# Loading x as columns, and its rows later, at the start of a two-layer decoder trunk

## The chip, the cores and the metric

One NeuronCore of a Trainium2 chip runs the whole program, one launch. The metric is the device time of that launch in microseconds, the median of several runs. A profiled execution is a run of its own, with its own time.

## The reference

Two layers over 256 tokens of width 1024, float32. Each layer is a half-step SwiGLU sub-layer, a token-mixing sub-layer (windowed attention and latent attention, gated), and a second half-step SwiGLU. The change touches the first SwiGLU of the first layer alone:

```
def rms_norm(x, g):
    y = x * rsqrt(mean(x * x, axis=-1) + 1e-6)
    return y * g
for l in range(2):
    x = x + 0.5 * (silu(h @ w_gate) * (h @ w_up)) @ w_down      # h = rms_norm(x, ffn1_norm[l])
    ...
```

w_gate and w_up are 1024 x 2816, w_down is 2816 x 1024.

## The kernel before

Every float32 operand of a matmul is split in two float32r parts, high (a rounded copy, made by ScalarE) and low (the rest, a subtraction on VectorE). A product is then three matmul passes: high by high, high by low, low by high. A SwiGLU runs over 22 blocks of 128 hidden columns. For a block the gate's and the up part's weights (a `gu` block, 1 MB) stand still in TensorE and the normalised x streams through. TensorE contracts over its partitions, so x has to lie with its 1024 channels on partitions: 8 "columns" of 128 channels by 256 tokens, in `hT` (high and low beside each other, so that one 512-wide matmul, `high`, does high weight by both parts of x; `low`, 256 wide, does low weight by high x). Only the gain goes into `hT`. The factor 1/rms of a token, `rs`, is left out there and comes in afterwards: `spread_rs` on TensorE (two transposes, L1410 to L1415) spreads it over the partitions, ScalarE copies it to `rsB` (L627 to L630), and VectorE multiplies the gate's sum by it (`gate_scaled`, L953). From there silu, the product with the up part, its split into `aTh` and `aTl`, and the twelve matmuls of the down block (`down`, L1576) follow.

At the program's start nothing is on the chip. SyncE issues all loads from one queue in the order of the code (L316 to L323, L360 to L362): x in two halves, with the gains (`cols`) in front of the first; block 0's weights in four pieces of 256 KB (`start_cols(i)`: gate or up by i % 2, channels 0 to 511 or 512 to 1023 by i // 2); block 1's in two pieces of 512 KB; block 0's down weights `d0`; block 2's weights into `SG` (`third_raw`); and `d1`. Later loads wait until VectorE has read the buffer that they fill.

x comes with tokens on partitions. TensorE therefore transposes it (`column_start`, L1396, 16 matmuls with the identity into PSUM), ScalarE makes the high part (`columns_high`, L610) and VectorE the low part (`columns_low`, L1006), both reading the transposed x from PSUM. Until x is there TensorE multiplies a constant (`keep_warm`, L1380). Each engine runs its instructions in the order in which the code issues them, and semaphores (`start_hi`, `ht_lo`, ...) tie the engines together. ScalarE's order is L705 to L719, VectorE's L1076 to L1083 and then `ffn`, TensorE's `gate_up_start` (L1523), `gate_up_second`, `gate_up_third`, `down`. In `gate_up_start` a group of four `high` matmuls (`start_high_four(s, half)`; s is 0 for gate, 1 for up) is followed by its four `low`.

The sum of squares of x is made from x by rows, on ScalarE (L718) and VectorE (L897). VectorE finishes the mean (L932, L934), GpSimd the power -1/2 (L465). `spread_rs` stands after the fifth `high` matmul of block 1's up part (L1553).

Of the kernel before, what the change touches and what calls it, by code (L numbers as in the profile page):

```python
# [14 lines left out]
P = 128  # L15
# [46 lines left out]
X_AT_FIRST = ((2, 0), (3, 0), (4, 0), (6, 0), (5, 0), (7, 0), (2, 1), (3, 1))  # L62
X_AT = ((2, 0), (3, 0), (4, 0), (6, 0), (2, 1), (3, 1), (5, 0), (7, 0))
RS_BANK = 5
COLS_PAD = 32
# [32 lines left out]
def build(nc, x_first_in, x_second_in, pos_in, cols_in, rows_in, w_ffn, w_proj, w_gate, w_uq, w_ukv, w_branch, w_out,  # L98
          masks_in, freq_in, out):
    with ExitStack() as ctx:  # L100
# [31 lines left out]
        qkB_PT = sb("qkB_PT", [P, 2 * TT * HB * QKB])  # L132
        qB = qkB_PT[:, 0:TT * HB * QKB].rearrange("p (t n) -> p t n", t=TT)
        kB_rows = qkB_PT[:, TT * HB * QKB:]
        kB = qkB_PT[:, TT * HB * QKB:].rearrange("p (t n) -> p t n", t=TT)
        PT = qkB_PT[:, :].rearrange("p (h n) -> p h n", h=HB)
# [18 lines left out]
        x_cols = sb("x_cols", [P, COLS_PAD + TT * D_MODEL])  # L155
        x = x_cols[:, COLS_PAD:].rearrange("p (h t n) -> p h t n", h=2, t=TT)
        cols = x_cols[:, 0:7 + 3 * KC]
# [51 lines left out]
        ht_ps = signal("ht_ps", 3 * KC)  # L209
# [14 lines left out]
        x_in_done = [signal(f"x_in_done{h}", 0) for h in range(2)]  # L224
# [81 lines left out]
        def x_place(layer, n, c):  # L306

            bank, half = (X_AT_FIRST if layer + n == 0 else X_AT)[c]
            return ps[:, bank, half * SEQ:(half + 1) * SEQ]
# [5 lines left out]
        def _(sp):  # L315
            part = slice(0, COLS_PAD + TT * HALF)  # L316
            sp.dma_start(x_cols[:, part], x_first_in).then_inc(x_in_done[0].sem, 16)  # L317
            sp.dma_start(x_cols[:, COLS_PAD + TT * HALF:], x_second_in).then_inc(x_in_done[1].sem, 16)  # L318
            for i in range(4):
                sp.dma_start(raw_gu[0][:, start_cols(i)], w_ffn[0, :, start_cols(i)]).then_inc(start_in[i].sem, 16)  # L320
            for s, sem in enumerate((start_in[4].sem, raw_gu_in[1].sem)):
                part = slice(s * KC * P, (s + 1) * KC * P)
                sp.dma_start(raw_gu[1][:, part], w_ffn[1, :, part]).then_inc(sem, 16)  # L323

# [24 lines left out]
            def load_ffn_first(l, w):  # L349
                for b in range(2):  # L350
                    if w == 1:
                        sp.wait_ge(lo_gu.sem, lo_gu.at(l, MIX0 + OUT + 1 + b))
                    elif l > 0:
                        sp.wait_ge(lo_gu.sem, lo_gu.at(l - 1, FFN2_0 + FB - 2 + b))
                    if l + w > 0:
                        load_gu((2 * l + w) * FB + b, b)
                    if l > 0 and w == 0 and b == 0:
                        load_last_d(l - 1, 1)
                if l == 0 and w == 0:
                    load_d(0, 0)  # L360
                    sp.dma_start(third_raw, w_ffn[2, :, 0:GU_COLS]).then_inc(third_in.sem, 16)
                    load_d(1, 1)  # L362
                    return
                for b in range(2):
                    if w == 1:
                        sp.wait_ge(lo_gu.sem, lo_gu.at(l, MIX0 + OUT + 3))
                    else:
                        sp.wait_ge(lo_d.sem, lo_d.at(l - 1, 2 * FB - 2 + b))
                    load_d((2 * l + w) * FB + b, b)
# [58 lines left out]
        def _(pool):  # L428
# [11 lines left out]
            pool.wait_ge(x_in_done[0].sem, 16)  # L440
            pool.sem_inc(small_in.sem, 16)
            pool.wait_ge(x_in_done[1].sem, 16)
# [77 lines left out]
        def _(act):  # L520
# [4 lines left out]
            for l in range(DEPTH):  # L525
# [80 lines left out]
                def columns_high(n, part=range(KC)):  # L606
                    act.wait_ge(small_in.sem, small_in.per_layer * (l + 1))
                    for c in part:
                        act.wait_ge(ht_ps.sem, ht_ps.at(l, KC * n + c))
                        act.activation(hTh[:, c, :], x_place(l, n, c), ACT.Copy,  # L610
                                       scale=cols[:, 7 + n * KC + c:8 + n * KC + c]).then_inc(ht_hi.sem, 1)
# [93 lines left out]
                if l == 0:  # L705
                    columns_high(0, range(0, 4))
                    start_high(0)
                    columns_high(0, range(4, 6))
                    start_high(1)
                    columns_high(0, range(6, 8))  # L710
                    start_high(2)
                    start_high(3)
                    for s, (landed, sig) in enumerate(((start_in[4], start_hi), (raw_gu_in[1], hi_gu))):
                        part = slice(s * KC * P, (s + 1) * KC * P)
                        act.wait_ge(landed.sem, 16)
                        act.activation(wh_gu[1][:, part], raw_gu[1][:, part], ACT.Copy).then_inc(sig.sem, 1)
# [152 lines left out]
        def _(dve):  # L869
# [3 lines left out]
            for l in range(DEPTH):  # L873
# [12 lines left out]
                def split_second(n):  # L886

                    for half, sig in enumerate((lo_first, lo_gu)):
# [7 lines left out]
                        if n + half == 0:  # L896
# [105 lines left out]
                def columns_low(n, part=range(KC), layer=l):  # L1002
                    dve.wait_ge(small_in.sem, small_in.per_layer * (layer + 1))
                    for c in part:
                        dve.wait_ge(ht_hi.sem, ht_hi.at(layer, KC * n + c))
# [361 lines left out]
        def _(pe):  # L1367
# [15 lines left out]
            keep_warm(7)  # L1383
            pe.wait_ge(ident_set.sem, 2)
            for l in range(DEPTH):
# [9 lines left out]

                def column_start(c):  # L1396

                    if c >= 6:
                        pe.wait_ge(ht_lo.sem, ht_lo.at(0, c - 6))
                    dst = x_place(0, 0, c)  # L1400
                    for t in range(TT):
                        ins = pe.transpose(dst[:, t * P:(t + 1) * P], x[:, c // 4, t, c % 4 * P:(c % 4 + 1) * P], ident[:, :])
                    ins.then_inc(ht_ps.sem, 1)
# [119 lines left out]
                def gate_up_start():  # L1523

                    pe.wait_ge(x_in_done[0].sem, 16)
                    for c in range(4):
                        column_start(c)
                    keep_warm(1)
                    pe.wait_ge(x_in_done[1].sem, 16)
                    for c in range(4, KC):  # L1530
                        column_start(c)
                    start_high_four(0, 0)
                    start_low_four(0, 0)
                    start_high_four(1, 0)
                    start_low_four(1, 0)
                    start_high_four(0, 1)
                    start_low_four(0, 1)
                    start_high_four(1, 1)
                    start_low_four(1, 1)

                def gate_up_second(w):

                    for s, sig in enumerate((gate_ps, gu_used)):
# [16 lines left out]
                        ins.then_inc(sig.sem, 1)  # L1560
                def gate_up_third():
# [423 lines left out]
```

## Time and profile before

| what | us |
|---|---|
| runs of the kernel before | 1039.35, 1039.02, 1038.98; median 1039.02 |
| the profiled execution's own time | 1039.14 |
| its span, first to last instruction | 1037.3 |
| TensorE (PE) busy with matmuls | 1032.0, 99% of the span |
| VectorE (DVE) busy | 717.8, 69% |
| ScalarE (ACT) busy | 586.5, 57% |
| GpSimd (POOL) busy | 65.5, 6% |
| loads: mean rate over the span | 181 GB/s, 187.53 MB |
| the first fortieth of the span, 25.9 us | 264 GB/s, engines of the DMA busy 7 tenths |

A busy time says how long an engine had something under way. A timeline row gives start, length, engine, line, operation and tiles (out<-in), how often, and in brackets how long the engine had been idle before and what ended that. The chain of waits follows the end of the program back to its start. A DMA row gives the time from issue to landing. The granted clock is TensorE's; it has two levels here, 1.00 (2.4 GHz) and 0.50 (1.2 GHz).

### The profile page before, as it was taken

The numbers are of one execution on the slowest core, as the hardware profiler recorded it, in microseconds if no ns is written. First come the engines' busy times: TensorE is split into PE (matmuls) and PEld (weight loads), VectorE is DVE, ScalarE is ACT, GpSimd is POOL, SyncE is SP. The second block draws the span as 40 slices with busy tenths as digits, with TensorE's granted clock in tenths as the row PEclk, the third lists the DMA queues.
The fourth block names the chain that finished last, engine by engine and source line by source line (L and its number), as shares of the span: only waits on it lengthen the run. The fifth ranks groups of instructions, "written<-read, shape, count | busy, mean of one in ns | idle before, by whom it ended". The sixth has DMA issues, their size and how long they took to land.

```text
span 1037.3 us, 15559 instructions
## 1 busy us (share of the span) xinstructions
PE 1032.0 (99%) x5648; PEld 892.2 (86%) x5648; DVE 717.8 (69%) x1132; ACT 586.5 (57%) x935; POOL 65.5 (6%) x71
## 2 busy tenths in 40 slices
PE   9999999999999999999999999999999999999998
PEld 7888888998888888888888888889988888888887
DVE  6766676668786876666687666666697868676665
ACT  7545454457864755454565455455688646454552
POOL 0052000122100000000000000001211000000000
PEclk9999999999999999999999999999999999999999
DMA  7665544455335555655545555634454346546551
GB/s 264 249 227 192 203 163 166 141 184 207 131 123 203 177 190 185 207 191 204 181 146 204 200 194 180 214 132 155 153 204 162 122 162 222 203 162 202 190 174 61
DMA packets 35269, 187.53 MB, mean 181 GB/s; under 512 B 4368, under 2 KB 4384, under 8 KB 20128
## 3 DMA queue, kind: packets, MB, share of 16 engines
q1 hardware_dynamic: 34992, 186.51, 51.6%
q0 software_dynamic: 240, 0.53, 0.2%
q8 instruction: 23, 0.38, 0.1%
q14 instruction: 14, 0.11, 0.0%
HBM read 185.98 MB, written 1.05 MB: 180 GB/s over the span
## 4 chain that ended last, share of the span: by engine, by line
PE 99%; DMA 1%; SPq 0%; DVE 0%; ACT 0%; issue 0%
PE ps L1369 96%; PE ps L1803 1%; PE ps L1393 1%; DMA w_raw<-in_w_ffn 1%; PE ps L1832 1%; PE ps L1868 0%; PE ps L1712 0%; PE ps L1704 0%; PE ps L1414 0%; DVE x_cols L999 0%; ACT w_hi L554 0%; SPq L318 0%; SPq L317 0%
## 5 line engine op out<-in xcount | busy, mean ns | idle before, releaser
L1369 PE MATMUL ps<-hT,w_hi 128*128 128x512 f32 x1408 | 341.2, 391 | 0.9 <-ACT w_hi L554 0.9
L1369 PEld LDWEIGHTS ps<-hT,w_hi 128*128 128x128 f32 x1408 | 258.9, 188 | 51.4 <-ACT w_hi L554 1.1
L884 DVE TENSOR_TENSOR w_lo<-w_raw,w_hi 128x2048 fp32r<-128x2048 f32 x82 | 188.0, 2292 | 87.4 <-ACT w_hi L549 87.4
L1369 PEld LDWEIGHTS ps<-hT,w_lo 128*128 128x128 f32 x1408 | 176.7, 188 | 7.5
L1369 PE MATMUL ps<-hT,w_lo 128*128 128x256 f32 x1408 | 178.3, 279 | 0.0
L1369 PE MATMUL ps<-w_hi,hT 128*128 128x512 f32 (+2 forms) x576 | 173.5, 376 | 0.0
L549 ACT ACTIVATE w_hi<-w_raw 128x2048 fp32r<-128x2048 f32 x85 | 161.9, 1905 | 13.6 <-PE ps L1369 13.2
L1369 PE MATMUL ps<-w_lo,aTh 128*128 128x512 f32 x352 | 137.1, 390 | 0.0
L1369 PE MATMUL ps<-w_hi,aTl 128*128 128x512 f32 x352 | 137.0, 389 | 0.0
L1369 PE MATMUL ps<-w_hi,aTh 128*128 128x512 f32 x352 | 136.8, 390 | 0.0
L578 ACT ACTIVATE S<-ps 128x256 f32<-128x256 f32 x88 | 33.7, 383 | 155.4 <-PE ps L1369 155.4
L1369 PEld LDWEIGHTS ps<-w_hi,hT 128*128 128x128 f32 x576 | 107.2, 188 | 14.8
L878 DVE TENSOR_TENSOR w_lo<-w_raw,w_hi 128x2048 fp32r<-128x2048 f32 (+3 forms) x50 | 94.8, 1903 | 29.8 <-ACT w_hi L537 29.6
L572 ACT ACTIVATE w_hi<-w_raw 128x1024 fp32r<-128x1024 f32 x88 | 92.8, 1055 | 38.5 <-PE ps L1369 38.5
L537 ACT ACTIVATE w_hi<-w_raw 128x2048 fp32r<-128x2048 f32 (+3 forms) x54 | 86.0, 1593 | 49.0 <-PE ps L1369 47.0
L1369 PE MATMUL ps<-w_lo,hT 128*128 128x512 f32 (+2 forms) x288 | 107.5, 373 | 0.0
L940 DVE TENSOR_TENSOR w_lo<-w_raw,w_hi 128x1024 fp32r<-128x1024 f32 x88 | 104.3, 1218 | 1.4 <-ACT w_hi L572 1.4
L946 DVE TENSOR_TENSOR S<-ps,S 128x256 f32<-128x256 f32 x88 | 37.0, 420 | 85.4 <-ACT S L578 85.4
L1369 PEld LDWEIGHTS ps<-w_hi,aTl 128*128 128x128 f32 x352 | 66.1, 188 | 13.9
L1369 PEld LDWEIGHTS ps<-w_hi,aTh 128*128 128x128 f32 x352 | 66.1, 188 | 13.6
L1369 PEld LDWEIGHTS ps<-w_lo,aTh 128*128 128x128 f32 x352 | 66.1, 188 | 13.0
L584 ACT ACTIVATE work<-work 128x256 f32<-128x256 f32 x88 | 36.7, 418 | 68.1 <-DVE work L953 68.1
(168 smaller groups left out, 956.9 us busy)
## 6 DMA issues: line engine op xcount, KB each, us to landing
w_raw<-in_w_ffn SPq DMA_DIRECT2D x85, 1024.0 KB, 5.0
w_raw<-in_w_ffn SPq DMA_DIRECT2D x90, 512.0 KB, 5.8
w_raw<-in_w_gate SPq DMA_DIRECT2D x16, 1024.0 KB, 4.9
w_raw<-in_w_proj SPq DMA_DIRECT2D x16, 592.0 KB, 4.3
w_raw<-in_w_branch SPq DMA_DIRECT2D x8, 1024.0 KB, 4.9
w_raw<-in_w_out SPq DMA_DIRECT2D x8, 1024.0 KB, 4.9
w_raw<-in_w_uq SPq DMA_DIRECT2D x4, 384.0 KB, 3.1
w_raw<-in_w_ffn SPq DMA_DIRECT2D x4, 256.0 KB, 6.2
```

The source lines that it names most:

```text
L537: act.activation(mix_hi[m][:, 0:ncols], mix_raw[m][:, 0:ncols], ACT.Copy).then_inc(hi_gu.sem, 1)
L549: act.activation(wh_gu[b], raw_gu[b], ACT.Copy).then_inc(hi_gu.sem, 1)
L572: act.activation(wh_d[b], raw_d[b], ACT.Copy).then_inc(hi_d.sem, 1)
L578: act.activation(folded[:, b, 0, :], ps[:, 2 * b, SEQ:2 * SEQ], ACT.Copy).then_inc(g_low.sem, 1)
L584: act.activation(silu[:, b, :], silu[:, b, :], ACT.Silu).then_inc(silu_done.sem, 1)
L878: dve.tensor_tensor(mix_lo[m][:, 0:ncols], mix_raw[m][:, 0:ncols], mix_hi[m][:, 0:ncols].bitcast(F32), ALU.subtract).then_inc(lo_gu.sem, 1)
L884: dve.tensor_tensor(wl_gu[b], raw_gu[b], wh_gu[b].bitcast(F32), ALU.subtract).then_inc(lo_gu.sem, 1)
L940: dve.tensor_tensor(wl_d[b], raw_d[b], wh_d[b].bitcast(F32), ALU.subtract).then_inc(lo_d.sem, 1)
L946: dve.tensor_tensor(folded[:, b, 0, :], ps[:, 2 * b, 0:SEQ], folded[:, b, 0, :], ALU.add)\
L1369: return pe.matmul(dst, w, m, start=start, stop=stop, skip_group_check=True)
L1393: ins = pe.transpose(dst[:, t * P:(t + 1) * P], x[:, c // 4, t, c % 4 * P:(c % 4 + 1) * P], ident[:, :])
L1803: ins = pe.transpose(ps[:, 4 + h % 4, s * P:(s + 1) * P], S[:, h, s * P:(s + 1) * P], ident[:, :])
```

## The change

The host lays x out a second time, as columns (`xt_first`, channels 0 to 511, with the gains behind it; `xt_second`, channels 512 to 1023). In the first sub-layer of the first layer, ScalarE and VectorE split these columns straight from SBUF; the 16 transposes, the PSUM places for them and their waits are gone there. `xt_first` goes out first, `xt_second` behind the first of block 0's four pieces. x by rows, 1024 KB in one load, goes out behind block 1's weights; both sums of squares wait for it, on VectorE now behind both halves of block 1's low part. Block 2's weights go out ahead of `d0`. ScalarE's order of columns and pieces changes, and VectorE's. TensorE runs two groups of `high` (gate, up) and then two of `low`, for each half of the channels, `spread_rs` stands behind the whole of block 1, and the constant is multiplied 10 times, not 7 and 1. The columns lie where `qB`, `kB` and `PT` are put later, and a pad moves those.

```diff
-        ht_ps = signal("ht_ps", 3 * KC)
+        ht_ps = signal("ht_ps", 3 * KC, -KC)
...
         def x_place(layer, n, c):
-            bank, half = (X_AT_FIRST if layer + n == 0 else X_AT)[c]
+            if layer + n == 0:
+                return xt(c)
+            bank, half = X_AT[c]
...
-            part = slice(0, COLS_PAD + TT * HALF)
-            sp.dma_start(x_cols[:, part], x_first_in).then_inc(x_in_done[0].sem, 16)
-            sp.dma_start(x_cols[:, COLS_PAD + TT * HALF:], x_second_in).then_inc(x_in_done[1].sem, 16)
+            sp.dma_start(xt_first, xt_first_in).then_inc(xt_in[0].sem, 16)
             for i in range(4):
+                if i == 1:
+                    sp.dma_start(xt_second, xt_second_in).then_inc(xt_in[1].sem, 16)
                 sp.dma_start(raw_gu[0][:, start_cols(i)], w_ffn[0, :, start_cols(i)]).then_inc(start_in[i].sem, 16)
...
+            sp.dma_start(x_cols[:, cols_at + COLS_PAD:], x_in).then_inc(x_in_done.sem, 16)
...
                 if l == 0 and w == 0:
+                    sp.dma_start(third_raw, w_ffn[2, :, 0:GU_COLS]).then_inc(third_in.sem, 16)
                     load_d(0, 0)
-                    sp.dma_start(third_raw, w_ffn[2, :, 0:GU_COLS]).then_inc(third_in.sem, 16)
                     load_d(1, 1)
...
-            pool.wait_ge(x_in_done[0].sem, 16)
+            pool.wait_ge(xt_in[0].sem, 16)
             pool.sem_inc(small_in.sem, 16)
-            pool.wait_ge(x_in_done[1].sem, 16)
+            pool.wait_ge(x_in_done.sem, 16)
             pool.sem_inc(x_done.sem, 2 * TT)
...
                 if l == 0:
-                    columns_high(0, range(0, 4))
+                    columns_high(0, range(0, 2))
                     start_high(0)
-                    columns_high(0, range(4, 6))
+                    columns_high(0, range(2, 4))
                     start_high(1)
-                    columns_high(0, range(6, 8))
+                    columns_high(0, range(4, 8))
                     start_high(2)
                     start_high(3)
...
                     act.wait_ge(ss_clear.sem, 1)
+                    act.wait_ge(x_in_done.sem, 16)
...
-                        if n + half == 0:
+                        if n == 0 and half == 1:
+                            dve.wait_ge(x_in_done.sem, 16)
...
                 if l == 0:
                     columns_low(0, range(0, 4))
                     start_low(0)
-                    columns_low(0, range(4, 6))
                     start_low(1)
-                    columns_low(0, range(6, 8))
+                    columns_low(0, range(4, 8))
                     start_low(2)
                     start_low(3)
...
-            keep_warm(7)
+            keep_warm(10)
...
                 def gate_up_start():
-                    pe.wait_ge(x_in_done[0].sem, 16)
-                    for c in range(4):
-                        column_start(c)
-                    keep_warm(1)
-                    pe.wait_ge(x_in_done[1].sem, 16)
-                    for c in range(4, KC):
-                        column_start(c)
-                    start_high_four(0, 0)
-                    start_low_four(0, 0)
-                    start_high_four(1, 0)
-                    start_low_four(1, 0)
-                    start_high_four(0, 1)
-                    start_low_four(0, 1)
-                    start_high_four(1, 1)
-                    start_low_four(1, 1)
+                    for half in range(2):
+                        for s in range(2):
+                            start_high_four(s, half)
+                        for s in range(2):
+                            start_low_four(s, half)
...
                             high(2 + s, wh_gu[1][:, c:c + P], k, k == 0)
-                            if l + w == 0 and s == 1 and k == 4:
-                                spread_rs(0)
...
+                    if l + w == 0:
+                        spread_rs(0)
```

`columns_high` and `columns_low` wait for the landing of the half that column c lies in (`xt_in[c // 4]`) where they waited for the transposes.

SyncE's queue from the program's start, before: x's two halves are ahead of all weights, and `SG` is block 2.

```order
L317 DMA x_cols<-in_x_first 128x1056
L318 DMA x_cols<-in_x_second 128x1024
L320 DMA w_raw<-in_w_ffn 128x512 x4
L323 DMA w_raw<-in_w_ffn 128x1024 x2
L347 DMA w_raw<-in_w_ffn 128x1024
L361 DMA SG<-in_w_ffn 128x2048
L347 DMA w_raw<-in_w_ffn 128x1024
```

The same queue now:

```order
L328 DMA x_cols<-in_xt_first 128x1056
L332 DMA w_raw<-in_w_ffn 128x512
L331 DMA x_cols<-in_xt_second 128x1024
L332 DMA w_raw<-in_w_ffn 128x512 x3
L335 DMA w_raw<-in_w_ffn 128x1024 x2
L336 DMA x_cols<-in_x 128x2048
L373 DMA SG<-in_w_ffn 128x2048
L360 DMA w_raw<-in_w_ffn 128x1024 x2
```

One weight piece has moved ahead of the second half of x, and 1024 KB have come in ahead of block 2 and both down blocks.

TensorE from its first matmul to the second group of `low`, before (`hT`,`w_hi` 512 wide is a `high`, `hT`,`w_lo` 256 wide a `low`):

```order
L1380 MATMUL ps<-kTA 128x128 [waits warm_set]
L1380 MATMUL ps<-kTA 128x128 x6
L1402 MATMUL ps<-ident,x_cols 128x128 [waits x_in_done0,ident_set]
L1402 MATMUL ps<-ident,x_cols 128x128 x7
L1380 MATMUL ps<-kTA 128x128
L1402 MATMUL ps<-ident,x_cols 128x128 [waits x_in_done1]
...
L1369 MATMUL ps<-hT,w_hi 128x512 [waits ht_lo,start_hi]
L1369 MATMUL ps<-hT,w_hi 128x512 [waits ht_lo] x3
L1369 MATMUL ps<-hT,w_lo 128x256 [waits start_lo]
L1369 MATMUL ps<-hT,w_lo 128x256 x3
L1369 MATMUL ps<-hT,w_hi 128x512 [waits start_hi]
```

The same place now:

```order
L1399 MATMUL ps<-kTA 128x128 [waits warm_set]
L1399 MATMUL ps<-kTA 128x128 x9
L1388 MATMUL ps<-hT,w_hi 128x512 [waits ht_lo,start_hi,ident_set]
L1388 MATMUL ps<-hT,w_hi 128x512 [waits ht_lo] x3
L1388 MATMUL ps<-hT,w_hi 128x512 [waits start_hi]
L1388 MATMUL ps<-hT,w_hi 128x512 x3
L1388 MATMUL ps<-hT,w_lo 128x256 [waits start_lo]
L1388 MATMUL ps<-hT,w_lo 128x256 x3
```

The transposes are gone, and the second group of `high`, with its wait for the second weight piece, stands ahead of the first `low`.

VectorE from block 0's last low piece to the first use of `rsB` (`S`,`rsB`), before:

```order
L894 TENSOR_TENSOR w_lo<-w_raw,w_hi 128x1024 [waits start_hi]
L897 SCALAR_TENSOR_TENSOR sq,ss<-x_cols 128x1024
L932 TENSOR_TENSOR rs_step<-ss 128x2 [waits ss_done]
L934 TENSOR_SCALAR rs_step<-rs_step 128x2 [waits ms_sum]
L894 TENSOR_TENSOR w_lo<-w_raw,w_hi 128x1024 [waits hi_gu]
L946 TENSOR_TENSOR S<-ps,S 128x256 [waits g_low]
L964 TENSOR_TENSOR S<-ps,S 128x256 [waits u_low]
L908 TENSOR_TENSOR w_lo<-SG,w_hi 128x1024 [waits third_hi]
L953 TENSOR_TENSOR work<-S,rsB 128x256 [waits gate_sum,rsb_done]
```

The same place now:

```order
L911 TENSOR_TENSOR w_lo<-w_raw,w_hi 128x1024 [waits start_hi]
L911 TENSOR_TENSOR w_lo<-w_raw,w_hi 128x1024 [waits hi_gu]
L915 SCALAR_TENSOR_TENSOR sq,ss<-x_cols 128x1024 [waits x_in_done]
L950 TENSOR_TENSOR rs_step<-ss 128x2 [waits ss_done]
L952 TENSOR_SCALAR rs_step<-rs_step 128x2 [waits ms_sum]
L964 TENSOR_TENSOR S<-ps,S 128x256 [waits g_low]
L982 TENSOR_TENSOR S<-ps,S 128x256 [waits u_low]
L926 TENSOR_TENSOR w_lo<-SG,w_hi 128x1024 [waits third_hi]
L971 TENSOR_TENSOR work<-S,rsB 128x256 [waits gate_sum,rsb_done]
```

The sum of squares has moved behind the second low half, and it waits for a load.

## Rows read from the trace of the kernel before

**Rows 1.** The page: busy time of each engine.

```profile
PE 1032.0 (99%) x5648; PEld 892.2 (86%) x5648; DVE 717.8 (69%) x1132; ACT 586.5 (57%) x935; POOL 65.5 (6%) x71
```

**Rows 2.** The chain of waits in order of time: start us, us, what.

```profile
1.65 5.90 DMA w_raw<-in_w_ffn
...
7.57 0.64 ACT w_hi L554
...
8.26 9.82 PE ps L1369 x53
```

**Rows 3.** Timeline, TensorE in the first block, the second, and a later one.

```profile
8.26 1.20 PE L1369 MATMUL ps<-hT,w_hi 128*128 128x512 f32 x4 [0.86 <-ACT w_hi L554]
...
13.96 2.03 PE L1369 MATMUL ps<-hT,w_hi 128*128 128x512 f32 x8
...
30.78 3.80 PE L1369 MATMUL ps<-hT,w_hi 128*128 128x512 f32 x16
...
34.42 2.03 PE L1369 MATMUL ps<-hT,w_lo 128*128 128x256 f32 x16
...
36.28 0.40 PE L1369 MATMUL ps<-w_hi,aTh 128*128 128x512 f32 x1
```

**Rows 4.** Timeline: when three of the first loads were issued.

```profile
1.18 0.43 SPq L318 DMA_DIRECT2D x_cols<-in_x_second  x1
...
2.12 0.43 SPq L320 DMA_DIRECT2D w_raw<-in_w_ffn  x1
...
5.54 0.65 SPq L361 DMA_DIRECT2D SG<-in_w_ffn  x1
```

**Rows 5.** DMA issues, these three: size, median us from issue to landing.

```profile
x_cols<-in_x_second SPq DMA_DIRECT2D x1, 512.0 KB, 4.5
...
w_raw<-in_w_ffn SPq DMA_DIRECT2D x1, 256.0 KB, 6.1
...
SG<-in_w_ffn SPq DMA_DIRECT2D x1, 1024.0 KB, 10.3
```

**Rows 6.** Timeline: TensorE's first transpose, at the landing of x's first half.

```profile
4.62 1.36 PE L1402 MATMUL ps<-ident,x_cols 128*128 128x128 f32 x8 [0.21 <-DMA x_cols<-in_x_first]
```

**Rows 7.** Groups by line, ACT and DVE, 0 to 17 us: busy us, mean ns.

```profile
L610 ACT ACTIVATE hT<-ps,x_cols 128x256 fp32r<-128x256 f32 x8 | 3.2, 472 | 3.2 <-PE ps L1402 3.2
L554 ACT ACTIVATE w_hi<-w_raw 128x512 fp32r<-128x512 f32 x4 | 2.4, 636 | 0.6 <-DMA w_raw<-in_w_ffn 0.6
...
L917 DVE TENSOR_TENSOR w_lo<-w_raw,w_hi 128x512 fp32r<-128x512 f32 x4 | 2.7, 685 | 0.6 <-ACT w_hi L554 0.6
```

**Rows 8.** The same work from SBUF: one line each, duration ns min/median/max.

```profile
L597 ACT ACTIVATE aTh<-work x88: 396/398/419, 20.7 to 1030.1; 128x256 fp32r<-128x256 f32 x88
...
L984 DVE TENSOR_TENSOR aTl<-work,aTh x88: 412/418/619, 21.8 to 1030.5; 128x256 fp32r<-128x256 f32 x88
```

**Rows 9.** Timeline: the chain of `rs`, and block 1's last split ahead of its `down`.

```profile
13.35 1.22 DVE L897 SCALAR_TENSOR_TENSOR sq<-x_cols 128x1024 f32<-128x1024 f32 x1
...
15.06 1.62 POOL L465 TENSOR_TENSOR rs<-rs_step,minus_half 128x2 f32<-128x2 f32 x1 [13.14 <-DVE rs_step L934]
...
17.91 0.38 PE L1414 MATMUL ps<-ident,rs 128*128 128x128 f32 x2
...
24.93 0.42 DVE L984 TENSOR_TENSOR aTl<-work,aTh 128x256 fp32r<-128x256 f32 x1
...
28.06 0.39 PE L1369 MATMUL ps<-w_hi,aTh 128*128 128x512 f32 x1
```

**Rows 10.** Timeline: TensorE's constants at the start, and its last matmul.

```profile
1.05 3.35 PE L1380 MATMUL ps<-kTA 128*128 128x128 f32 x14 [1.05 <-DVE kTA L870]
...
5.82 0.39 PE L1380 MATMUL ps<-kTA 128*128 128x128 f32 x2
...
1033.74 0.39 PE L1369 MATMUL ps<-w_hi,aTl 128*128 128x512 f32 x1
```

**Rows 11.** Windows at the end: engines' busy us, granted clock, DMA share, GB/s.

```profile
1036.10:1037.30 1.20, 0.00 (x0) 0.00 (x0) 0.00 (x0) 0.00 (x0) 0.00 (x0) 0.50 0.31 119
```

More of the change, by code:

```diff
@@ L61 @@
 Q_BANK, K_BANK = (4, 5, 6), (7, 0, 1)
-X_AT_FIRST = ((2, 0), (3, 0), (4, 0), (6, 0), (5, 0), (7, 0), (2, 1), (3, 1))
 X_AT = ((2, 0), (3, 0), (4, 0), (6, 0), (2, 1), (3, 1), (5, 0), (7, 0))
 RS_BANK = 5
-COLS_PAD = 32
+COLS_PAD, PT_FRONT, PT_BACK = 32, 48, 16
+PT_COLS = 2 * TT * HB * QKB
 PROJ_GROUPS = ((0, 384), (384, 768), (768, PROJ_COLS))
@@ L95, in at, with build @@
         return layer * self.per_layer + (k + 1 + self.first)
-def build(nc, x_first_in, x_second_in, pos_in, cols_in, rows_in, w_ffn, w_proj, w_gate, w_uq, w_ukv, w_branch, w_out,
+def build(nc, xt_first_in, xt_second_in, x_in, pos_in, cols_in, rows_in, w_ffn, w_proj, w_gate, w_uq, w_ukv, w_branch, w_out,
           masks_in, freq_in, out):
@@ L131, in build @@
         kTA = sb("kTA", [P, SEQ])
[L132 to L136, printed above, removed]
         qTB = sb("qTB", [P, 6, SEQ])
@@ L154, in build, with xt @@
         trig = sb("trig", [P, 2, TT, 16])
-        x_cols = sb("x_cols", [P, COLS_PAD + TT * D_MODEL])
-        x = x_cols[:, COLS_PAD:].rearrange("p (h t n) -> p h t n", h=2, t=TT)
-        cols = x_cols[:, 0:7 + 3 * KC]
+        x_cols = sb("x_cols", [P, PT_FRONT + PT_COLS + PT_BACK + COLS_PAD + TT * D_MODEL])
+        qkB_PT = x_cols[:, PT_FRONT:PT_FRONT + PT_COLS]
+        qB = qkB_PT[:, 0:TT * HB * QKB].rearrange("p (t n) -> p t n", t=TT)
+        kB_rows = qkB_PT[:, TT * HB * QKB:]
+        kB = qkB_PT[:, TT * HB * QKB:].rearrange("p (t n) -> p t n", t=TT)
+        PT = qkB_PT.rearrange("p (h n) -> p h n", h=HB)
+        cols_at = PT_FRONT + PT_COLS + PT_BACK
+        x = x_cols[:, cols_at + COLS_PAD:].rearrange("p (h t n) -> p h t n", h=2, t=TT)
+        cols = x_cols[:, cols_at:cols_at + 7 + 3 * KC]
+        xt_first = x_cols[:, cols_at - KC // 2 * SEQ:cols_at + COLS_PAD]
+        xt_second = x_cols[:, PT_FRONT:PT_FRONT + KC // 2 * SEQ]
+        def xt(c):
+            half, i = divmod(c, KC // 2)
+            return (xt_first, xt_second)[half][:, i * SEQ:(i + 1) * SEQ]
         rows = sb("rows", [P, 2 * ROPE + HA])
@@ L223, in build @@
         rows_in_done = signal("rows_in_done", 16)
-        x_in_done = [signal(f"x_in_done{h}", 0) for h in range(2)]
+        xt_in = [signal(f"xt_in{h}", 0) for h in range(2)]
+        x_in_done = signal("x_in_done", 0)
         start_in = [signal(f"start_in{i}", 0) for i in range(5)]
@@ L608, in columns_high @@
                     for c in part:
-                        act.wait_ge(ht_ps.sem, ht_ps.at(l, KC * n + c))
+                        if l + n == 0:
+                            act.wait_ge(xt_in[c // (KC // 2)].sem, 16)
+                        else:
+                            act.wait_ge(ht_ps.sem, ht_ps.at(l, KC * n + c))
                         act.activation(hTh[:, c, :], x_place(l, n, c), ACT.Copy,
@@ L1004, in columns_low @@
                     for c in part:
+                        if layer + n == 0:
+                            dve.wait_ge(xt_in[c // (KC // 2)].sem, 16)
                         dve.wait_ge(ht_hi.sem, ht_hi.at(layer, KC * n + c))
@@ L1394, in transposed @@
                         ins.then_inc(ht_ps.sem, 1)
[L1396 to L1403, printed above, removed]
                 def columns(layer, n, h):
@@ L1959 @@
     cols = gain_cols[0]
-    x_halves = a["x"].reshape(TT, P, 2, HALF).transpose(2, 1, 0, 3).reshape(2, P, TT * HALF)
+    x_rows = a["x"].reshape(TT, P, 2, HALF).transpose(1, 2, 0, 3).reshape(P, TT * D_MODEL)
+    xt_halves = a["x"].reshape(SEQ, 2, KC // 2, P).transpose(1, 3, 2, 0).reshape(2, P, KC // 2 * SEQ)
     arrays = {
-        "x_first": np.concatenate([cols, np.zeros((P, COLS_PAD - cols.shape[1]), f32), x_halves[0]], axis=1),
-        "x_second": x_halves[1],
+        "xt_first": np.concatenate([xt_halves[0], cols, np.zeros((P, COLS_PAD - cols.shape[1]), f32)], axis=1),
+        "xt_second": xt_halves[1],
+        "x": x_rows,
         "positions": a["positions"],
```

## The prediction

> **What bounds the kernel now.** I read the page's engine shares first: TensorE has a matmul under way in 99% of the span, every other engine has room [rows 1]. The chain of waits, from its start, says where TensorE is not yet the bound: a weight load until 7.55 us, ScalarE's high part of that piece until 8.21, and from 8.26 on TensorE alone [rows 2]. So only what comes before 8.26 us, and a new wait behind it, can change the time. The timeline then tells how full TensorE is in block 0: 16 `high` and 16 `low` run from 8.26 to 13.96, 5.70 us; with nothing to wait for, in a later block, 16 `high` take 34.42 - 30.78 = 3.64 and 16 `low` 36.28 - 34.42 = 1.86, together 5.50 [rows 3]. Block 0 thus stalls 0.20 us in all, and the whole head that can be won is the 8.26 us ahead of it.
>
> **The loads.** The sum of bytes in front of a load sets when it lands. Block 0's second piece (gate and up alternate, so it is the first up piece) has 528 + 512 + 256 + 256 = 1552 KB up to its end and lands at 2.12 + 6.1 = 8.2 us; block 2's weights end at 4624 KB and land at 5.54 + 10.3 = 15.8 [rows 4, 5]. That is 3072 KB in 7.6 us, 0.64 us for 256 KB, 2.55 for 1024. x's first half was there just ahead of 4.62 [rows 6], its second at 1.18 + 4.5 = 5.7 [rows 4, 5]. The first piece, 256 KB behind that, landed only at 7.55 [rows 2]: 1.9 us where the rate makes it 0.64, so some 1.2 us were lost there once.
>
> In the new order the first piece ends at 784 KB. At the rate alone it lands 0.64 us behind 4.5, at 5.1; with the same loss, at 6.3. The second half of the columns ends at 1296 KB, and the second piece again at 1552 KB: the same sum as before, and I take the same landing, **8.2 us**. (If the loss is gone, 7.0. I take the row of the same sum, since the piece that lost the time still comes first among the weights.) Everything up to block 1's weights keeps its sum. x by rows ends at 4112 KB: 15.8 - 512 KB (1.27) = 14.6 us. Block 2 ends at 5136 KB instead of 4624, +1.3, 17.1 us; `d0` about 18.4, `d1` 19.7.
>
> The Trainium skill, "DMA: Bandwidth & Descriptors", section "Latency and other measured facts", puts the access latency of HBM at 0.2 us on average and up to 2 us at high load. By that the 1.2 us are of a size that the load on the memory alone could make, at any place of the queue; no row here says which it was.
>
> **TensorE's block 0.** The 16 transposes and their PSUM reads go, but they ended ahead of 8.26 beside the load, so on the path they cost nothing by themselves. ScalarE's columns now come from SBUF: a 128x256 copy there takes 398 ns against 472 from PSUM, VectorE's 128x256 two-input operation 418 [rows 7, 8]. One after the other they start some 0.3 to 0.35 us apart (estimate: the duration less the 0.1 that neighbours overlap). Step by step: the columns are there at 4.5; GpSimd passes the gains' signal on, which I put at 0.2 us (no row shows it exposed; it only has to be ready by 5.4). ScalarE makes columns 0 and 1 until 5.5, waits for the first piece (5.1 to 6.3), needs 0.64 for it [rows 7]: TensorE's first real matmul starts at 5.9 to **7.0**, against 8.26. Columns 2 and 3 follow on ScalarE and VectorE until 8.2. Then comes the second piece: landing 8.2, high part 8.2 to 8.9. TensorE's second group waits for that, and since the new order puts it ahead of the first `low`, they wait behind it too. From 8.9 there is left: 12 `high` at 3.64/16 and 16 `low` at 1.86/16 [rows 3], 2.73 + 1.86 = 4.6, end at **13.5**, if ScalarE and VectorE keep ahead. ScalarE: columns 4 to 7 until 10.2, third piece until 10.8, fourth until 11.3; TensorE wants them at 10.7 and 11.6. VectorE: 0.685 for a piece [rows 7], low second piece until 9.6, columns until 11.0, last low piece until 12.2, wanted at 13.0. Both fit within 0.2 us. Gain: 13.96 - 13.5 = **0.4 to 0.5 us**. So what is won at the front is mostly taken back by the second piece, whose landing the change does not move.
>
> **The sum of squares and `rs`.** VectorE now waits for x until 14.6, and its low part of block 1 stands ahead of that wait, so nobody on TensorE waits for it. Queued behind are the folds of block 0's sums, first wanted by block 2's matmuls at 19. Squares 14.6 to 15.8 (1.22); from their end to GpSimd 15.06 - 14.57 = 0.5; the power 1.62 [rows 9]: `rs` at 17.9. TensorE comes to `spread_rs` behind block 1, 13.5 + 5.5 = 19.0. It has 1.1 us to spare: cost nothing; if x lands over 1.1 us later than 14.6, that is late next. The two transposes themselves (0.38) [rows 9] are moved, not removed. Block 2's weights, 17.1, are split by 18.2 for its first `high` at 19.2: cost nothing, 1 us to spare.
>
> Moved behind block 1, `rsB` comes 19.0 - 17.91 = 1.1 us later [rows 9], while TensorE is 0.45 earlier. The chain that hangs on it ends in `aTl` of block 1, done at 25.35, wanted by its `down` at 28.06 [rows 9]: 2.7 us to spare become 1.15. Cost nothing. The 1024 KB more delay `d0` by 5 us and `d1` by 2.6, which were 6 and 4 us early at ScalarE; the loads behind them are released by VectorE's reads and come about 1 us later, with several us to spare at TensorE.
>
> **The sum.** -0.45 us, nothing added. The profiled execution took 1039.14 us, 1.8 more than its span and 0.12 more than the median of 1039.02; against the median the forecast is **1038.6 us**. Less than 0.2% (2.08 us, about what a measurement of this kernel can tell from no change) either way.
>
> **The rivals.**
> *The second piece lands early.* If the 1.2 us were the place's and not the piece's, it lands at 7.0, TensorE is full from 7.7 and ends block 0 at 12.3: -1.6, **1037.4**. x then lands at 13.4, `rs` at 16.7, `spread_rs` is wanted at 17.8. Block 2, 15.9, just fits. For it: the rate before and behind is even. Against it: the slow place lies where the weights begin. With a part of the loss, times between 1037.4 and 1038.6. Chance 0.20.
>
> *TensorE's clock falls at the start.* Place: between the constants and block 0. Now the constants (14 rows in 3.35 us, 0.24 each, while two of the same at 5.82 take 0.39 together) and the transposes keep TensorE busy until 0.86 us ahead of 8.26 [rows 3, 10]. With the change 20 rows of constants end at about 5.7, and from there to 8.9 TensorE does four `high`, under 1 us of work. The trace's end shows a fall: the last matmul ends at 1033.74 + 0.39 = 1034.1, and in the window from 1036.1 the granted clock is 0.50, 1.2 GHz [rows 10, 11]. So some 2 us without a matmul were enough there. It decides if the first piece lands at 6.3, not at 5.1. Price: at the start TensorE worked some 4 us at the slow pitch before it went up [rows 10]; as long again from 8.9 does 2 us less work, block 0 ends at 15.5, +1.55, **1040.5**; a shorter fall gives 1039.5, and all of block 0 at the slow clock (+4.6 - 0.45) 1043.2. Against it: those were idle us, here some work lies in between. Chance 0.30.
> The Trainium skill, "TensorE: Matmul & The Clock Gate", section "HAM oscillation — how this bites in real kernels", has this case: a TensorE that waits for loads between short bursts of matmuls falls back to the half clock and pays at each burst. The trace's end agrees that it falls, 1036.1; whether bursts prevent it no row shows.
>
> *`rsB` comes too late.* The 1.15 us at block 1's `down` and the 1.1 at `spread_rs` are both worked out from loads that have not run in this order. If x lands 2 us late, TensorE stalls 0.9 at `spread_rs` and 0.5 to 1 at that `down`: +1.1, **1040.1**. Against it: the loads' rate is even. Chance 0.08.
>
> **How the numbers follow.** Forecast 0.40 (own range 1038.1 to 1039.0), early second piece 0.20, clock 0.30, late `rsB` 0.08, none of these 0.02. From 1037.3 to 1040.7 the range leaves out the worse half of the clock's case and little at the lower end. Faster by over 0.2% (under 1036.9) needs more than the largest gain that I can work out, 1.6: 0.03. Slower by over 0.2% (over 1041.1) needs the clock's worst end or two late chains: 0.06. Within: 0.91.
>
> **What would show it.** Right: the second piece's high part starts at about 8.2 and TensorE's second group at 8.9, block 1 begins at 13.5, x lands near 14.6, GpSimd's power starts at 16.3, `spread_rs` waits for nothing, `down` of block 1 neither, and the granted clock stays 1.00. `high` matmuls some 0.43 apart behind 8.9 would show the clock's case; the second piece at 7.0 the early one; idle time of TensorE ahead of `spread_rs` or that `down` the late one. Wrong altogether: a gain or a loss that arises behind 30 us, where I see the same work with time to spare.

## The result, and the profile after

| | before | changed |
|---|---|---|
| median of 22 runs each, us | 1038.99 | 1040.61 |
| lowest and highest | 1038.09, 1040.09 | 1038.67, 1042.39 |
| profiled execution, span, us | 1037.3 | 1039.4 |

The changed kernel is slower: ratio 1.0015, 95% interval 1.0009 to 1.0022. That is within the 0.2% called "no change", and within the range, but on the other side of the forecast of 1038.6.

The runs of the changed kernel lie 3.7 us apart, those of the kernel before 2.0, and the mean granted clock of a run sorts them: 5 runs at 1.000 have a median of 1039.42, 14 at 0.998 one of 1040.68, 3 at 0.996 one of 1042.10. Of the 55 runs of the kernel before beside the experiments, two took 1415 and 2106 us and are left out of every comparison; the others list a clock of 1.000, one of them 0.999.

The page, engines' shares: TensorE is as busy as before [rows 1], over a longer span.

```profile
PE 1031.9 (99%) x5636; PEld 892.0 (86%) x5636; DVE 718.5 (69%) x1132; ACT 587.4 (57%) x935; POOL 64.6 (6%) x71
```

The chain of waits from the start (start us, us, what) still begins with a weight load and goes on with TensorE [rows 2], but the load is now the second piece, and it lands at 9.05.

```profile
2.12 6.93 DMA w_raw<-in_w_ffn
...
9.07 0.64 ACT w_hi L567
...
9.76 12.02 PE ps L1388 x60
```

The timeline of TensorE in block 0 and at block 1's first matmul answers to [rows 3]:

```profile
1.05 3.91 PE L1399 MATMUL ps<-kTA 128*128 128x128 f32 x20 [1.05 <-DVE kTA L887]
...
5.93 0.70 PE L1388 MATMUL ps<-hT,w_hi 128*128 128x512 f32 x2 [0.97 <-DVE hT L1026]
...
6.87 0.90 PE L1388 MATMUL ps<-hT,w_hi 128*128 128x512 f32 x2 [0.24 <-DVE hT L1026]
...
9.76 1.19 PE L1388 MATMUL ps<-hT,w_hi 128*128 128x512 f32 x4 [1.99 <-ACT w_hi L567]
...
12.43 2.87 PE L1388 MATMUL ps<-hT,w_hi 128*128 128x512 f32 x8
...
15.13 1.10 PE L1388 MATMUL ps<-hT,w_lo 128*128 128x256 f32 x8
...
16.08 1.99 PE L1388 MATMUL ps<-hT,w_hi 128*128 128x512 f32 x8
```

The first real matmul starts 2.3 us earlier than before, and block 1 begins 2.1 us later, at 16.08 against 13.96. The eight `high` from 12.43 take 2.7 us until the next group; at the pace of [rows 3] they take 1.8. The windows say why (busy us of PE, PEld, DVE, ACT, POOL, then the granted clock, DMA share, GB/s):

```profile
8.00:9.00 1.00, 0.00 (x0) 0.00 (x0) 0.00 (x0) 0.00 (x0) 0.00 (x0) 1.00 1.06 418
9.00:10.00 1.00, 0.24 (x1) 0.24 (x2) 0.26 (x1) 0.93 (x2) 0.00 (x0) 1.00 1.03 418
10.00:10.80 0.80, 0.80 (x5) 0.63 (x5) 0.80 (x3) 0.80 (x3) 0.00 (x0) 1.00 1.06 435
10.90:14.20 3.30, 3.30 (x14) 2.91 (x13) 3.18 (x6) 3.30 (x6) 0.00 (x0) 0.50 1.03 436
14.30:15.00 0.70, 0.70 (x5) 0.56 (x4) 0.70 (x2) 0.00 (x0) 0.00 (x0) 1.00 1.00 421
```

From 10.9 to 14.2 us the granted clock is 0.50, 1.2 GHz. Ahead of that TensorE had ended its constants at 4.96 and had then done four `high`, with waits of 0.97 and 0.24 us, until it stood still for 2 us (to 9.76).

Behind block 0 nothing changed. From block 1's first `high` to the end of the span it is 1037.3 - 13.96 = 1023.3 us before and 1039.4 - 16.08 = 1023.3 now. So the whole question is when block 0 ends.

The loads, issue to landing, answer to [rows 5]; they were issued at 1.65, 2.12 and 4.98 us:

```profile
x_cols<-in_xt_second SPq DMA_DIRECT2D x1, 512.0 KB, 6.7
...
w_raw<-in_w_ffn SPq DMA_DIRECT2D x1, 256.0 KB, 6.9
...
x_cols<-in_x SPq DMA_DIRECT2D x1, 1024.0 KB, 10.4
```

The first weight piece, issued at 1.18, took 3.7 us and landed at 4.9, so nothing was lost on it. The columns' second half lands at 8.4, 3.5 us behind it, where the rate gives 1.3. The slow stretch has moved to that load and grown, and everything behind is 0.8 us late: second piece 9.05 (forecast 8.2), x 15.4 (14.6).

### The profile page after: what moved, and what is told of

Read it like the earlier page. It is cut to its first block, busy times and chain, and to the rows that moved or that the text cites. A ratio compares the mean times of both kernels' runs of the same rounds, so it can differ in the third digit from the quotient of the medians.

```text
span 1039.4 us, 15542 instructions
## 1 busy us (share of the span) xinstructions
PE 1031.9 (99%) x5636; PEld 892.0 (86%) x5636; DVE 718.5 (69%) x1132; ACT 587.4 (57%) x935; POOL 64.6 (6%) x71
## 4 chain that ended last, share of the span: by engine, by line
PE 99%; DMA 1%; SPq 0%; DVE 0%; ACT 0%; issue 0%
PE ps L1388 96%; PE ps L1804 1%; PE ps L1412 1%; DMA w_raw<-in_w_ffn 1%; PE ps L1833 1%; PE ps L1869 0%; PE ps L1713 0%; PE ps L1705 0%; PE ps L1424 0%; DVE x_cols L1017 0%; ACT w_hi L567 0%; SPq L332 0%; SPq L331 0%; SPq L328 0%
```

## The experiments

Two theories stood against each other. **Theory 1**: the clock falls, since TensorE has too little to do while it waits for the second piece, and the late landing costs 0.4 us besides. **Theory 2**: the new order of the groups, waiting for the late piece, is the whole loss. A separate pair, A and B, is about the slow stretch in the loads. All kernels below are the changed one with the edit shown; each was compared with the kernel before in the same session.

### e1_fill: keep TensorE at work while it waits

```diff
-            keep_warm(10)
+            keep_warm(12)
...
                             start_high_four(s, half)
+                            if half + s == 0:
+                                keep_warm(8)
```

> The changed kernel with constants multiplied 12 times at the start and 8 times more between TensorE's first and second group of block 0, where it waits 2 us for the second weight piece. Theory 1 (the clock falls because TensorE does too little between 5 and 9.8 us, worth 3.41 us at half speed = 1.7 us): granted clock 1.00 up to the last matmul in every run, block 0 ends at 14.4 instead of 16.1, median 1039.2 to 1039.5. Theory 2 (the order of the groups and the late second piece alone cost the time): nothing gained, 1040.6.

Measured: 1039.54 (11 runs, 1039.10 to 1039.85), ratio 1.0007, interval 0.9998 to 1.0016. Ten runs have a mean clock of 1.000, one 0.999. The same windows as above:

```profile
10.00:10.80 0.80, 0.80 (x7) 0.75 (x6) 0.80 (x3) 0.80 (x3) 0.00 (x0) 1.00 1.08 446
10.90:14.20 3.30, 3.30 (x21) 2.80 (x20) 3.19 (x6) 2.74 (x4) 0.00 (x0) 1.00 1.02 428
```

TensorE's second group, and block 1's first:

```profile
9.22 1.17 PE L1388 MATMUL ps<-hT,w_hi 128*128 128x512 f32 x4
...
14.16 2.01 PE L1388 MATMUL ps<-hT,w_hi 128*128 128x512 f32 x8
```

21 matmuls run in the stretch where the changed kernel has 14. Theory 1 holds and Theory 2 falls: the queue and the order of the groups are those of the changed kernel, the only edit is work that nobody uses, and 1.07 us are back. (In this profile the second piece landed at 8.45, not 9.05, so that 14.16 is no test of the 14.4 expected; the five runs of the changed kernel whose clock stayed up, 1039.42, are as fast as these.) The constants fill two waits, the one ahead of TensorE's first real matmul and the one for the second piece; which of the two the clock needed, this run does not tell. The 0.6 us left over the kernel before lie within this run's interval.

### e2_alternate: high and low alternating again

```diff
                             start_high_four(s, half)
-                        for s in range(2):
                             start_low_four(s, half)
```

> The changed kernel with high and low groups alternating again, as in the kernel before. Theory 1: the first low group (0.47 us, its operand is ready at 7.83) moves into the 2 us wait for the second piece, so 0.5 us less from that; whether the clock then still falls is open, since only 0.5 us more work lies ahead of 9.8: 1040.1 if it falls, 1039.0 if not. Theory 2 (the order of the groups is the whole loss): back to the kernel before, 1039.0 with the clock as it was in the changed kernel.

Measured: 1039.48 (1038.35 to 1040.84), ratio 1.0008, 0.9999 to 1.0017. Ten of 11 runs have a clock of 1.000 (median 1039.40), one 0.998 (1040.84). So the one `low` group in the wait is mostly enough to keep the clock, and the median lies between the two values given for Theory 1. By itself this run does not tell the theories apart, and one run at 0.998, 1.4 us above that median, is too little to do so. Its profile had the second piece early, at 7.5, and block 0 ended at 13.21:

```profile
5.87 1.84 PE L1388 MATMUL ps<-hT,w_hi 128*128 128x512 f32 x4 [0.18 <-DVE hT L1026]
7.81 0.74 PE L1388 MATMUL ps<-hT,w_lo 128*128 128x256 f32 x4
8.39 1.09 PE L1388 MATMUL ps<-hT,w_hi 128*128 128x512 f32 x4
...
13.21 2.03 PE L1388 MATMUL ps<-hT,w_hi 128*128 128x512 f32 x8
```

The `low` at 7.81 runs where the changed kernel waits. The span was 1036.5, 1023.3 behind block 0's end again, the shortest of all profiles. That is no gain over the kernel before: the profiled run took 1038.35, and 6 of the 31 runs of the kernel before made beside it were as short (1038.02 to 1038.35).

### e3_issue_late: issue fewer loads at once

```diff
+            sp.wait_ge(start_in[1].sem, 16)
             for s, sem in enumerate((start_in[4].sem, raw_gu_in[1].sem)):
```

> The changed kernel, SyncE waits for the landing of the second weight piece before it issues block 1's weights and all behind. Theory A (loads that are still being issued slow the ones under way: the slow packets end when SyncE has issued its last load, 6.7 us before and 7.5 us with the change): the columns' second half lands at 6.2, the second piece at 6.9, block 0 ends near 12.5, 1037.5 to 1038. Theory B (the slow stretch belongs to the time since the start, or to the third load of the queue): they land at 8.4 and 9.05 as before, block 1 a little later, 1040.6 or more.

Measured: 1040.53 (1039.19 to 1041.73), ratio 1.0017, 1.0008 to 1.0026; 3 of 11 runs at a clock of 1.000 (median 1039.31), 7 at 0.998 (1040.80), one at 0.996 (1041.73). The third and fourth load (issued at 1.65 and 2.12) took as long as ever:

```profile
x_cols<-in_xt_second SPq DMA_DIRECT2D x1, 512.0 KB, 6.4
...
w_raw<-in_w_ffn SPq DMA_DIRECT2D x1, 256.0 KB, 6.6
```

They landed at 8.0 and 8.7, not at 6.2 and 6.9. Theory A falls: that the slow packets end when the last load is issued was a coincidence.

This profile is one in which the clock stayed up:

```profile
9.39 1.18 PE L1389 MATMUL ps<-hT,w_hi 128*128 128x512 f32 x4 [1.69 <-ACT w_hi L568]
...
14.40 2.01 PE L1389 MATMUL ps<-hT,w_hi 128*128 128x512 f32 x8
...
9.40:14.40 5.00, 5.00 (x29) 4.29 (x29) 4.21 (x8) 4.22 (x8) 0.00 (x0) 1.00 0.95 342
```

TensorE had waited 1.7 us ahead of 9.39 and done the same four `high` as in the changed kernel, and the granted clock was 1.00 all the same; in the other 8 of 11 runs of this kernel it was lower. How long TensorE waited in those is not on record, and what decides whether the clock falls, no run here shows.

### e4_piece_early: the second weight piece ahead of the columns' second half

```diff
-                if i == 1:
+                if i == 2:
                     sp.dma_start(xt_second, xt_second_in).then_inc(xt_in[1].sem, 16)
```

> The changed kernel with the columns' second half behind the second weight piece instead of ahead of it. If the slow stretch (2.2 us lost) hits whatever is under way from 4.5 to 7 us, the second piece lands at 7.4 to 7.8 instead of 9.05 and the second group starts at 8.4 instead of 9.76; the columns' second half lands at 9.05 and the third group waits for it until 10.9: block 0 gains 0.6 us. Theory 1: 1040.0 if the clock still falls, 1038.6 if it does not. Theory 2: 1040.0.

Measured: 1039.06 (1038.35 to 1041.55), ratio 1.0003, 0.9994 to 1.0012. Eight of 11 runs at 1.000, with a median of 1039.05; the others 1038.66 (0.999), 1039.84 (0.998), 1041.55 (0.996). The second group started at 8.37, as expected:

```profile
6.79 0.90 PE L1388 MATMUL ps<-hT,w_hi 128*128 128x512 f32 x2 [0.24 <-DVE hT L1026]
8.37 1.65 PE L1388 MATMUL ps<-hT,w_hi 128*128 128x512 f32 x4 [0.69 <-ACT w_hi L567]
...
14.69 1.99 PE L1388 MATMUL ps<-hT,w_hi 128*128 128x512 f32 x8
...
9.00:12.20 3.20, 3.20 (x13) 2.92 (x12) 2.54 (x7) 3.14 (x7) 0.00 (x0) 0.50 1.05 424
```

This profile was one with a fall, and block 0 ended at 14.69, though no wait of TensorE behind the constants was longer than 0.7 us. Falls were rarer with the shorter wait, 2 of 11 runs against 17 of 22, which had been left open; the gain with the clock up, 1039.42 to 1039.05, was some 0.4 (5 and 8 runs), not the 0.8 that 1038.6 meant.

### e5_combined and e6_combined_order: what the above points to

Edits of e2_alternate and e4_piece_early, and constants in the two gaps; e6_combined_order changes ScalarE's order too.

```diff
-            keep_warm(10)
+            keep_warm(12)
...
                     for half in range(2):
+                        if half == 1:
+                            keep_warm(3, 3)
                         for s in range(2):
                             start_high_four(s, half)
-                        for s in range(2):
                             start_low_four(s, half)
...
# e6_combined_order alone
-                    columns_high(0, range(4, 8))
+                    columns_high(0, range(4, 6))
                     start_high(2)
+                    columns_high(0, range(6, 8))
                     start_high(3)
```

> The changed kernel with three edits together: second weight piece ahead of the columns' second half, high and low groups alternating, constants 12 times at the start and 3 times (into another bank) between the two halves of the channels. In all six profiles so far the span is block 0's end plus 1023.3 to 1023.4 us. Second piece at 7.7, columns' second half at 9.0, third group behind ScalarE's third piece at 10.9, block 0's end at 13.6 with the clock at 1.00: span 1037.0, time 1038.8 in every run. If the clock fell for another reason than idle TensorE, some runs stay at 1040 and above.

Measured: 1038.84 (1038.29 to 1039.09), ratio 1.0001, 0.9992 to 1.0010, every run at a clock of 1.000, span 1037.0 and block 0's end at 13.66, all three as forecast. The kernel before measured 1038.67 in the same session.

```profile
8.74 1.09 PE L1388 MATMUL ps<-hT,w_hi 128*128 128x512 f32 x4
9.67 0.63 PE L1388 MATMUL ps<-hT,w_lo 128*128 128x256 f32 x4
10.13 0.83 PE L1399 MATMUL ps<-kTA 128*128 128x128 f32 x6
10.76 1.19 PE L1388 MATMUL ps<-hT,w_hi 128*128 128x512 f32 x4
...
13.66 2.01 PE L1388 MATMUL ps<-hT,w_hi 128*128 128x512 f32 x8
```

> As e5_combined, and ScalarE splits the third weight piece between columns 5 and 6 instead of behind column 7. Theory: the third group starts when the third piece and column 4 are ready, 10.4 instead of 10.9, and the fourth column is the next wait: block 0's end 0.2 to 0.4 us earlier than in e5_combined, 1038.5. If VectorE's low columns are what the group waits for, no difference.

Measured: 1038.98 (1038.29 to 1039.72), ratio 1.0005, 0.9996 to 1.0014: no gain. The third group started earlier, at 10.33, but took longer:

```profile
10.33 1.39 PE L1389 MATMUL ps<-hT,w_hi 128*128 128x512 f32 x4
11.82 0.74 PE L1389 MATMUL ps<-hT,w_lo 128*128 128x256 f32 x4
...
10.28 0.88 DVE L1027 SCALAR_TENSOR_TENSOR hT<-x_cols,hT 128x256 fp32r<-128x256 f32 x2 [0.41 <-ACT hT L626]
```

Its last matmul waits for VectorE's last low column, done at 11.16, and the end, 13.81, is no earlier. That is the second case of the expectation. So with the clock kept and the order mended, the change comes out even with the kernel before and not ahead of it.

### e7_split_first, e8_loads_later, e9_small_first: where the slow stretch belongs

```diff
# e7_split_first
-            sp.dma_start(xt_first, xt_first_in).then_inc(xt_in[0].sem, 16)
+            for part in (slice(0, 2 * SEQ), slice(2 * SEQ, KC // 2 * SEQ + COLS_PAD)):
+                sp.dma_start(xt_first[:, part], xt_first_in[:, part]).then_inc(xt_in[0].sem, 16)
# e8_loads_later
+            sp.wait_ge(silu_ready.sem, 1)
             sp.dma_start(xt_first, xt_first_in).then_inc(xt_in[0].sem, 16)
# e9_small_first
+            sp.dma_start(freq[:, :], freq_in).then_inc(freq_landed.sem, 16)
+            sp.dma_start(rows[:, :], rows_in[0:1, :].to_broadcast([P, 2 * ROPE + HA])).then_inc(rows_in_done.sem, 16)
             sp.dma_start(xt_first, xt_first_in).then_inc(xt_in[0].sem, 16)
```

> The changed kernel, the first load cut in two (256 KB and 272 KB), the sum of bytes unchanged. If the slow stretch belongs to the third load of the queue, it is now the first weight piece that is slow: it lands at 6 or later instead of 4.9. If it belongs to the time since the start (some 4.1 to 7 us), the first piece lands at 4.9 as before and the columns' second half at 7.5 to 8.4.

> The changed kernel, SyncE issues its first load some 1.5 us later (behind ScalarE's first activation). If the slow stretch belongs to the time since the start (4.1 to 7 us), it hits the first load and the first weight piece: the piece lands at 8 rather than 6.4, and the columns' second half follows it in 1.3. If it belongs to the place in the queue, the first piece lands at 6.4 and the columns' second half 2.9 to 3.5 us behind it.

> The changed kernel with two small loads (8 KB and 36 KB, wanted much later) issued ahead of the columns' first half, which is now third in the queue and issued 0.95 us later. If the slow stretch belongs to the third load of the queue, the columns' first half takes 1 to 2 us longer (lands at 6 to 7 instead of 5.2) and the columns' second half lands 1.3 us behind the first weight piece. If it begins when the first load has landed (it did so within 0.5 us in every profile so far), it begins near 3 us and hits the columns' first half just as well; if it belongs to the bytes under way (the first 800 to 1000 KB), the columns' first half lands at 5.2 and its second half again 2.8 to 3.5 us behind the first piece.

One execution each: 1040.52, 1042.65 and 1040.87 us. The loads of e7_split_first; the second half of the first load was issued at 1.18, the first piece at 1.65, the columns' second half at 2.12:

```profile
x_cols<-in_xt_first SPq DMA_DIRECT2D x1, 272.0 KB, 3.0
...
w_raw<-in_w_ffn SPq DMA_DIRECT2D x1, 256.0 KB, 4.6
...
x_cols<-in_xt_second SPq DMA_DIRECT2D x1, 512.0 KB, 5.5
```

They land at 4.2, 6.2 and 7.6: the first piece, now third, takes 2.0 us behind the load ahead of it (0.6 at the rate), the columns 1.4 (1.3 at the rate). In e8_loads_later the first piece was issued at 2.69 and the columns at 3.17:

```profile
w_raw<-in_w_ffn SPq DMA_DIRECT2D x1, 256.0 KB, 3.7
...
x_cols<-in_xt_second SPq DMA_DIRECT2D x1, 512.0 KB, 6.0
```

Landings 6.4 and 9.2, 2.8 us apart: the slow stretch came 1.5 us later along with the loads. In e9_small_first the columns' first half was issued third, at 1.65, the first piece at 2.12, the columns' second half at 2.59:

```profile
x_cols<-in_xt_first SPq DMA_DIRECT2D x1, 528.0 KB, 5.3
...
w_raw<-in_w_ffn SPq DMA_DIRECT2D x1, 256.0 KB, 5.6
...
x_cols<-in_xt_second SPq DMA_DIRECT2D x1, 512.0 KB, 6.4
```

The first half lands at 6.95, the second 1.3 us behind the first piece. The load ahead of the first half was

```profile
rows<-in_gain_rows SPq DMA_DIRECT2D x1, 36.0 KB, 4.3
```

issued at 1.18 and landed at 5.5. So in this run the slow load was the second, 36 KB in 3.1 us behind the first (landed at 2.4), and the third followed it in 1.4 where the rate gives 1.3. With one execution each, the three speak against the time since the start (in e8_loads_later the first piece came 0.6 us behind the load ahead of it, at 6.4), against one piece, and against the bytes under way (in e7_split_first the slow load ends at 784 KB, which came at the rate in the changed kernel). e7_split_first and e8_loads_later agree with the third place in the queue; e9_small_first bears it out by the landing that was forecast, but not by which load was slow. Whether it is the place, or the time since the first load landed, or in e9_small_first the small load itself, they do not tell apart. That stays open. The clock fell in all three; in e8_loads_later it was down longest, from 8.6 to 15.5 us, and its mean over the run was the lowest, 0.997.

## Why the prediction was wrong

**What bounds the kernel: right.** All that changed lies ahead of block 1; 1023.3 to 1023.4 us behind it are the same in both kernels and in the profiles of all nine experiments.

**The second piece at 8.2 us: this step failed.** The prediction took "the same landing" for the same sum of bytes, and the loss of 1.2 us to belong to the first weight piece, "since the piece that lost the time still comes first among the weights". The first piece lost nothing; the third load did, 512 KB now where it was 256, and the loss was 2.2 us. The second piece landed at 9.05. With the 4.6 us counted from TensorE's second group that makes 9.76 + 4.6 = 14.4, 0.4 later than before instead of 0.45 earlier. The 4.6 were short too, since they let TensorE wait for nothing behind its second group: with the clock up that stretch took 4.9 us in e1_fill (9.22 to 14.16) and 5.0 in e3_issue_late (9.39 to 14.40), part of it a wait for the high part of the third piece. The 5 runs whose clock stayed at 1.000 agree: 1039.42 against 1038.99. So do the runs with the clock up of e1_fill, e2_alternate and e3_issue_late, in which the second piece stays behind the columns (medians 1039.54, 1039.40 and 1039.31, the kernel before at 1038.97), and of e4_piece_early, in which it does not (1039.05); these are few runs each, sorted by their clock, and no interval goes with them. e2_alternate has the old order of the groups and is not clearly faster than the others, which points to the landing and not to the order.

**"The clock stays": this choice failed.** The rival was there, with its place and a chance of 0.30. Its price was 2 us of work lost at the slow clock, less the 0.45 won: +1.55, 1040.5. In the profile block 0 ended at 16.08, 2.1 later than before. By e1_fill's and e3_issue_late's 4.9 and 5.0 us it would have ended near 14.7 with the clock up (an estimate), which leaves 1.4 to the fall and 0.7 to the late piece and the waits behind it; over the runs, the 14 at a clock of 0.998 lie 1.3 above the 5 at 1.000. That the median, 1040.61, came so near to 1040.5 is in part luck: a gain counted that was a loss, and a fall priced higher than it was. The row of the trace's end [rows 10, 11] had shown a fall, and the text set against it that here some work lies in between: in 17 of 22 runs that work was not enough. It was said to decide "if the first piece lands at 6.3, not at 5.1". The piece landed early, at 4.9, and the clock fell all the same: the stretch with little work ran from 4.96, where the constants ended (forecast 5.7), to 9.76 (forecast 8.9). That too little work in between is the cause, e1_fill shows; how little is too little it does not, since e3_issue_late's profile kept the clock over a wait of 1.7 us and e4_piece_early's lost it with none over 0.7. The Trainium skill, "TensorE: Matmul & The Clock Gate", section "HAM oscillation — how this bites in real kernels", describes this fall between bursts that wait for loads; the trace agrees, with a clock of 0.50 from 10.9 to 14.2.

**The early second piece, 1037.4: half right.** e2_alternate's profile had it at 7.5, not 7.0, and a span 0.8 us below that of the kernel before, not 1.6. With the same queue it landed at 9.05 in the changed kernel's profile and at 8.45 in e1_fill's; one profile of the kernel before could not tell such a spread.

**Columns from SBUF: mis-sized.** They were priced at 398 ns after a copy from SBUF [rows 8]; ScalarE needs more for them than for those from PSUM [rows 7]:

```profile
L626 ACT ACTIVATE hT<-x_cols 128x256 fp32r<-128x256 f32 x8 | 3.5, 497 | 2.2 <-POOLq L454 2.2
```

It costs some 0.1 us each: columns 4 to 7 took 1.7 us (9.61 to 11.31), where the sum had 1.3, and the third piece behind them on ScalarE came that much later. With the clock up TensorE waits 0.1 to 0.2 us for it, as said above. GpSimd's pass of the gains' signal, put at 0.2 us with no row behind it, took no more: the columns landed at 4.2 (issued at 0.74, 3.5 us) and ScalarE started at 4.40.

**`rs`, its later place, block 2 and the down blocks: right.** TensorE came to `spread_rs` at 21.6, waited for nothing, and went on 0.13 us later. It was itself 2.6 us later than forecast, which alone could hide a late `rs`; but `rs` was done at 18.05 (forecast 17.9), ahead of the forecast's 19.0 as well. That this came so near is luck: x was 0.8 us late, and GpSimd's power took 0.72 us, where the sum had the 1.62 of the kernel before:

```profile
17.33 0.72 POOL L478 TENSOR_TENSOR rs<-rs_step,minus_half 128x2 f32<-128x2 f32 x1 [15.41 <-DVE rs_step L952]
...
21.62 0.38 PE L1424 MATMUL ps<-ident,rs 128*128 128x128 f32 x2
...
21.75 2.10 PE L1388 MATMUL ps<-hT,w_hi 128*128 128x512 f32 x8
...
28.64 0.42 DVE L1002 TENSOR_TENSOR aTl<-work,aTh 128x256 fp32r<-128x256 f32 x1
...
30.15 0.39 PE L1388 MATMUL ps<-w_hi,aTh 128*128 128x512 f32 x1
```

`aTl` of block 1 was done at 29.06 and wanted at 30.15: 1.1 us to spare, forecast 1.15. The late-`rsB` rival did not happen.

## What to carry to other kernels

Work that TensorE does while it waits (here the transposes and a `low` group) may be worth more than its own length: taking it away cost the clock in 17 of 22 runs here, and the matmuls behind paid for it. Where a change opens a wait on TensorE, look for the next fall of the granted clock in the trace, price it, and fill the wait with work that nobody uses, as e1_fill did, or close it by order. And a landing is no function of the bytes ahead alone: give it the spread that the trace's slowest load shows before a gain of half a microsecond rests on it.

## What the runs showed of the hardware that was not expected

One of the first loads of SyncE's queue was slow at the start in every kernel whose loads are shown here. It was the third in most: 1.9 us where 0.64 is the rate in the kernel before, 3.5 where it is 1.3 in the changed one, 2.0 for 0.64 in e7_split_first; in e9_small_first it was the second. In one execution each it moved with the queue and not with time, and its size varies; in e5_combined's profile a part fell on the second load already (landing 5.5, at the rate 4.7). What sets it stays open. A scaled copy of 128x256 from SBUF took 497 ns on ScalarE where the same from PSUM took 472. And the runs of the changed kernel fell into groups, with medians 1.3 and 1.4 us apart, one for each further 0.002 of the mean granted clock.
